# Latent attention on one core: the values of the step behind ahead of the step's transposes, with a GEMM slice between them

## What is computed

```
# latent attention ("mla"), in each of 2 layers: 528 tokens, 8 heads, 96 wide
s = einsum('bqhd,bkhd->bhqk', qi, k) * scale
s = where(k_pos <= q_pos, s, NEG_BIG)
p = softmax(s, axis=-1)
o = einsum('bhqk,bkhd->bqhd', p, v)
# indexed attention ("dsa"), once: 512 tokens, 8 heads, 64 wide, one shared key/value head
_, idx = lax.top_k(iscore, 128)      # the keys that each query may see
logits = einsum('bqhd,bqkd->bhqk', q, k[idx]) * a_scale
o = einsum('bhqk,bqkd->bqhd', softmax(logits), v[idx])
```

## Time and profile before

| | us |
|---|---|
| three runs | 3520.9, 3518.26, 3521.11 |
| median | 3520.9 |
| the profiled execution | 3517.67 |
| its span | 3515.9 |

### The profile page before, as it was taken

The page is one execution under the profiler, slowest core; times in us unless marked ns, Lnnn a source line. Parts: engine busy times, 40 slices in busy tenths (PEclk is TensorE's granted clock), DMA queues, the critical chain, the costliest instruction groups (busy, mean ns, idle before and its releaser), DMA issues.

```text
span 3515.9 us, 66728 instructions
## 1 busy us (share of the span) xinstructions
PE 3365.1 (96%) x26596; PEld 3267.6 (93%) x26596; DVE 1415.4 (40%) x2183; ACT 1065.7 (30%) x1502; POOL 1278.9 (36%) x589
## 2 busy tenths in 40 slices
PE   7999989999999999999989999999998878999999
PEld 7999979898999999999979998999997776799999
DVE  4121343487521123121343587422136697452212
ACT  3222332322332233222333323322233334343222
POOL 3444432122444444343432122443342550144443
PEclk9999999999999999999999999999999996899999
DMA  3333322133333323333221233333323422133333
GB/s 121 90 90 90 87 60 55 46 95 104 96 90 90 90 84 91 90 90 89 78 65 50 55 90 110 96 90 90 90 86 94 99 68 88 32 101 96 90 96 96
DMA packets 544884, 299.47 MB, mean 85 GB/s; under 512 B 23280, under 2 KB 528624, under 8 KB 544560
## 3 DMA queue, kind: packets, MB, share of 16 engines
q1 hardware_dynamic: 514128, 258.77, 26.0%
q10 hardware_dynamic: 30560, 37.99, 3.3%
HBM read 278.49 MB, written 17.04 MB: 84 GB/s over the span
## 4 chain that ended last, share of the span: by engine, by line
issue 59%; POOL 22%; PE 13%; DVE 4%; POOLq 1%; ACTq 0%; ACT 0%; DVEq 0%
POOL wl L433 22%; PE pair L529 13%; POOLq L432 1%; DVE tmp L1658 0%; POOLq L437 0%; DVE negt L1737 0%; DVE negt L1727 0%; DVE top L1736 0%; ACTq L1183 0%; DVE negt L1725 0%; DVE tmp L1656 0%; DVE tmp L1644 0%; PE aux L863 0%; ACTq L1218 0%; DVE tmp L1787 0%
## 5 line engine op out<-in xcount | busy, mean ns | idle before, releaser
L433 POOL TENSOR_TENSOR wl<-raw,wh 128x1024 fp32r<-128x1024 f32 (+4 forms) x549 | 1218.8, 2222 | 2219.3 <-ACT wh L906 2212.2
L529 PE MATMUL pair<-xh,wh 128*128 128x264 f32 (+1 forms) x5200 | 1080.2, 289 | 34.9 <-POOL wl L433 18.4
L529 PE MATMUL pair<-xl,wh 128*128 128x264 f32 (+1 forms) x5200 | 1058.5, 285 | 0.0
L529 PE MATMUL pair<-xh,wl 128*128 128x264 f32 (+1 forms) x5200 | 1057.4, 285 | 0.0
L529 PEld LDWEIGHTS pair<-xh,wh 128*128 128x128 f32 x5200 | 810.6, 190 | 50.9 <-issue 23.8
L529 PEld LDWEIGHTS pair<-xl,wh 128*128 128x128 f32 x5200 | 809.2, 189 | 0.0
L529 PEld LDWEIGHTS pair<-xh,wl 128*128 128x128 f32 x5200 | 808.0, 190 | 0.0
L906 ACT ACTIVATE wh<-raw 128x1024 fp32r<-128x1024 f32 (+4 forms) x549 | 527.4, 963 | 434.1 <-DMA raw<-ffn_w_down 160.6
L529 PE MATMUL pair<-ah,wh 128*128 128x264 f32 (+1 forms) x2312 | 478.1, 288 | 22.1 <-DVE R L1496 7.0
L1280 DVE TENSOR_TENSOR tmp<-pair,rstd 128x528 f32<-128x528 f32 (+1 forms) x222 | 156.2, 704 | 842.1 <-PE pair L529 840.3
L529 PE MATMUL pair<-al,wh 128*128 128x264 f32 (+1 forms) x2312 | 473.1, 286 | 0.0
(11 more groups left out here) (294 smaller groups left out, 2772.4 us busy)
## 6 DMA issues: line engine op xcount, KB each, us to landing
raw<-ffn_w_gu SPq DMA_DIRECT2D x176, 512.0 KB, 3.8
raw<-w_in SPq DMA_DIRECT2D x103, 512.0 KB, 3.9
raw<-ffn_w_down SPq DMA_DIRECT2D x64, 512.0 KB, 3.7
raw<-ffn_w_down SPq DMA_DIRECT2D x32, 384.0 KB, 3.2
raw<-w_out SPq DMA_DIRECT2D x24, 512.0 KB, 3.7
raw<-w_ffn_gate SPq DMA_DIRECT2D x22, 512.0 KB, 3.8
raw<-w_ffn_up SPq DMA_DIRECT2D x22, 512.0 KB, 3.8
gate_scratch<-gst ACTq DMA_DIRECT2D x32, 264.0 KB, 2.7
```

The source lines that it names most:

```text
L433: nc.gpsimd.tensor_tensor(wl[:, k % SPL, 0:n], raw[:, k % SPL, 0:n], wh[:, k % SPL, 0:n].bitcast(F32), ALU.subtract).then_inc(S["split_don ...
L529: mm = nc.tensor.matmul(pp[:, h, 0:th], w[:, s, kk * P:(kk + 1) * P], x[:, kk, t0 + h * th:t0 + (h + 1) * th], start=(kk == 0 and n == 0), ...
```

## The change

In PE's part of `attention`, and nowhere else, two calls change places around the second place of the step:

```diff
                     if between is not None:
                         between(n)
-                    turn(n)
+                    if n >= 1:
+                        values(n - 1)
                     if after is not None:
                         after(n)
-                    if n >= 1:
-                        values(n - 1)
+                    turn(n)
                     if n >= 2 and (n - 2) % HEADS == HEADS - 1:
                         turn_out((n - 2) // HEADS)
```

## The result

| | before | after |
|---|---|---|
| median, us (4 runs each) | 3519.87 | 3564.64 |
| range, us | 3518.26 to 3521.11 | 3557.12 to 3566.07 |
| the profiled execution, us | 3517.67 | 3557.12 |

The ratio is 1.0123, its 95% interval 1.0106 to 1.0141: the change makes the kernel 1.2% slower. The forecast was 3563.7 us.

What follows compares the result with a forecast made beforehand. PE, busy 96% of the span and in order, was taken as the bound; 40.8 us for two latent attentions plus 2 for the indexed one gave 3560.5 us, or 3563.7 us as median, range 3546 to 3590.

Steps and rivals of the forecast that it cites:

- The sum: Whole kernel: 20.4 us per latent layer, 40.8 for two, plus 2 in the indexed attention, 42.8 us slower.
- One wait at 528 keys: Latent steps at 528 keys: PE waits 1.22 us behind transposes for their copies; eight such waits, 9.8 us per layer.
- turn_out of the three tiles before: Latent steps 9, 17, 25: turn_out right behind the transposes waits for the copies, 2.9 us per layer.
- Unit ends: Latent steps with n mod 3 = 2: DVE's evacuation stands behind the later copies, so PE waits; 7.5 us per layer.
- Small ones: Latent attention, per layer: values fill waits for HF and gst, -0.7 us; three waits for normalise add 0.9 us.
- The indexed attention: Indexed attention: values move into waits for the exponential, but ACT is the bound; +2 us, from -5 to +6.
- the last values once, 0.65 us: Indexed attention: the last values wait for the copies once, costing 0.65 us.
- Rival 1: Latent attention: the clock falls behind the 1.22 us waits, +25.6 us, 3589 us in all; chance 0.16.
- Rival 2: Latent attention: only the waits at 528 keys come out, 19.6 us, 3540 us in all; chance 0.07.
- Rivals 3 and 4: 3: values fill indexed attention's exponential waits, 5 us faster, 3516, chance 0.05. 4: later waits absorb all, no change, 3521, 0.04.

Runs made afterwards that it cites:

- e7_evac_first: Changed kernel, but DVE evacuates a GEMM unit ending in the second place ahead of the step's copies; 3551.27 us, ratio 1.0100 to the kernel before.
- e8: Kernel before, with values ahead of transposes only in indexed-attention steps 11 to 14, 20, 21 and latent step 24; 3512.36 us, ratio 0.9989.
- e2: Kernel before, with the new order in the indexed attention alone; 3522.75 us, ratio 1.0011 to the kernel before.
- e5_longer_copies: Changed kernel, with DVE also filling an unread 128x512 tile ahead of each latent step's copies; 3594.81 us, ratio 1.0234 to the kernel before.
- e4_old_order_528: Changed kernel, but the old order from step 32 on (528 keys) in the latent attentions; indexed kept the new order; 3538.85 us, ratio 1.0055.
- e1: Kernel before, with the new order in the two latent attentions alone; 3559.36 us, ratio 1.0118 to the kernel before.

## Why the prediction was right

**The sum.** It had 42.8 us on the profiled execution; the three stretches grew by 43.3. The median of after is 44.8 us over that of before. The profiled execution itself grew by 39.5; 2.5 us of the difference to 43.3 is the shorter time between the attentions, the rest lies ahead of the first. That the median came within 1 us of the forecast is luck: the four executions of after lie between 3557 and 3566 us. Inside the 43.3 us errors offset each other too. The clock at the start of the latent stretches cost after 2.5 us and before 4.6; without it their growth is 20.3 and 20.7 us, 41.0 in all. Of this 2.0 us is the clock in the last values, which the sum left out, so the waits make 39.0 us where the prediction had 40.8. And the indexed attention took 2.4 us more than its term.

**One wait at 528 keys, 1.22 us.** It measured 1.21. Working from start to start was what made it right: the waits' list shows 0.97 for the same event. The eight of them, 9.8 us, measured 9.0 per layer; the steps from 32 on grew by 10.1 and 10.0 us because the clock added 1.0.

**turn_out of the three tiles before, 2.9 us.** The list has 3.4 us for four turn_outs; with 0.24 us each for what hides in the transposes' length (1.21 less 0.97) that is 4.4, and less 1.2 for turn_out(3) it leaves 3.2. Right, slightly low.

**Unit ends, 7.5 us.** The list has ten waits, 7.2 us, but three of them stood before too, with 1.3 us, so 5.9 us are new there. The one at 400 keys shown above costs 0.82 us from start to start (617.20 plus the scores' 0.79 to 618.81), 0.1 more than the list says and less than the prediction's 1.0. By subtraction, the growth ahead of step 32 is 10.3 and 10.7 us without the start's clock; less 3.2 for turn_out that leaves 7.1 and 7.5 for unit ends and the small ones together, where the prediction had 7.7. Right in size, slightly high. e7_evac_first showed that these waits come from DVE's order.

**Small ones, +0.2 in sum.** The wait for HF was filled where values stood ahead of it, as e8 shows; the waits for normalise, taken at 0.9 us in three places, are 0.5 us in two in the list of after.

**The indexed attention, +2 in -5 to +6.** Measured +4.4 (after) and +4.2 (e2). Inside the range, but this is the term that was mis-sized, and the step that failed in it is "the last values once, 0.65 us". Its end after, in PE's timeline:

```profile
3098.93 0.61 PE L617 MATMUL aux<-con,tmp 128*128 128x128 f32 x4
3100.32 1.10 PE L630 MATMUL aux<-R,tmp 128*128 128x64 f32 x8 [0.78 <-DVE tmp L1384]
...
3102.65 1.30 PE L630 MATMUL aux<-R,tmp 128*128 128x64 f32 x8 [0.78 <-DVE tmp L1384]
3105.07 1.09 PE L639 MATMUL aux<-con,tmp 128*128 128x128 f32 x4 [1.11 <-DVE tmp L1395]
```

And before:

```profile
3062.63 2.05 PE L630 MATMUL aux<-R,tmp 128*128 128x64 f32 x16
3065.80 0.63 PE L639 MATMUL aux<-con,tmp 128*128 128x128 f32 x4 [1.11 <-DVE tmp L1395]
```

Before, the values of steps 30 and 31 ran in one piece behind turn(31), and values(30) covered the copies for values(31). After, both values(30) and values(31) stand right behind transposes, because the last step has no scores and no GEMM unit: from the last scores to the last turn_out 11.4 us in place of 9.3, 2.1 us of the 4.4. The prediction saw this doubling in latent attention and missed it here. The rest is turn_out of step 25 (1.1 us), 0.7 us in steps 28 to 30, and 0.5 us that had built up by step 25. The waits for the exponential there, after, with the three turn_outs ("issue": the profile names no releaser):

```profile
PE aux L617 <- ACT tmp L1016: 7.8, 6, 1.6
PE aux L630 <- DVE tmp L1384: 2.5, 3, 0.9
PE aux L639 <- issue: 2.1, 3, 0.8
```

The waits for the exponential shrank by 1.5 us from the earlier trace rows and bought nothing, as the prediction expected from ACT's table loads.

**The rivals.** Rival 1, the clock, happened only in the last step of each latent attention, for 1.0 us of time: after is at 1.00 in all windows of its two latent attentions but the first and last. It wasn't an empty one: e5_longer_copies made it happen in between too, with the same waits 0.45 us longer, and e4_old_order_528 shows one such fall with waits as short as those of after, so that after was spared it is in part luck. Rival 2 (only the waits at 528 keys) would have left +19.6 us; e4 and e7 show the other half. Rivals 3 and 4 are refuted by e1 and e2.

**What isn't settled.** In e5_longer_copies the longest waits, behind 2001 us, left the clock at 1.00 (the row at 2021 above), while shorter ones at 1885 us (1.13 us) and 626 us (1.19 us) stood ahead of a fall, and so did the 0.79 us in e4_old_order_528. So the length of the single wait doesn't decide alone. What does, these runs don't tell.

## What to carry to other kernels

On an engine that takes its instructions in order, look behind each producer for what stands between it and the first instruction that needs what others make of its result: that stretch is its cover, and a reordering that moves it ahead of the producer brings the round trip into the open (here 1.21 us: from PE free behind the transposes, through two copies on VectorE, to PE's restart) wherever such a reader comes next: at 21 places in 40 steps here, not at each. Give the last steps of a loop their own count, since the work that separates producer and reader in the others is missing there. And read such a wait from start to start, because the list of waits leaves out what lies under the modelled end of the matmul ahead.

## What the runs showed of the hardware

With after's waits of up to 1.1 us, 21 per latent attention, TensorE's granted clock stayed at 1.00 between the first 10 us and the last step. In the last step, behind two waits of 0.97 us about 3 us apart, it fell to half. With the same waits at up to 1.5 us it fell two and four times more per latent attention, for about 3.4 us each, and that cost 3.4 and 6.9 us. There is no clean border between the two: e4_old_order_528 has one such fall behind a wait of 0.79 us.

The Trainium skill ("TensorE: Matmul & The Clock Gate", "A second HAM failure mode: psum-queue depth-cycling") says of a bf16 kernel that frequent short idles of PE between groups of matmuls make the clock swing between its levels. This case's traces agree in part: e5_longer_copies shows such a swing, most waits of after passed without one.

The first 10 us of a latent attention, from its first scores, differ from execution to execution by the granted clock, and the runs show no cause in the kernel: it was 0.72 and 0.82 before, 0.75 and 1.00 after, and 1.00 in both layers of e4_old_order_528, whose order there is that of after. Lost are 2.8 and 1.8 us before against 2.5 and 0.0 after. A comparison of single traces to a microsecond has to take that out first: with it, the growth of the two latent attentions is 20.3 and 20.7 us.
